# Softmax heads of groups A and C in pairs, on rows and columns of the TensorE array

## The chip, the cores and the metric

The kernel runs on one core of a Trainium2 chip. Five engines work beside each other, each through its own list of instructions: TensorE (PE; its weight loads are shown as PEld), VectorE (DVE), ScalarE (ACT), GpSimd (POOL) and SyncE (SP, which only issues DMAs here). Semaphores tie them together. The metric is the device time of one execution in microseconds (us).

## The reference, cut to what matters

One layer of a streaming encoder for 512 prompt tokens and 64 sample tokens (these with 256 cached keys). After a norm and one wide projection, three groups of heads run: A is sparse attention, B stick-breaking, C differential. The change touches A and C, whose heads have 64 features:

```python
# A, 4 heads (keys outside the chosen top-k count as masked)
logits = einsum('bthd,btkhd->bhtk', q, kg) * HEAD_DIM ** -0.5
logits = logits - slopes * dist                     # ALiBi
p = softmax(where(valid, logits, -inf)); out = p @ vg
# C, 6 heads, two maps n = 0, 1 of 32 features each
logits = einsum('bthnd,bshnd->bnhts', q, k) * DIFF_QK ** -0.5
logits = where(allowed, logits - slopes * dist, -inf)
p = softmax(logits);  w = p[:, 0] - lam * p[:, 1];  out = w @ v
oc = rmsnorm(oc) * subln * (1 - lam_init)           # per head
```

Then come the output projection with a gated residual, a router, and a mixture of 64 small experts (the longest stage, not touched). Everything is fp32; a matmul in fp32 shows in the trace as two MATMUL records, each with its own weight load.

## The kernel before, in words

The queries stand in 5 tiles: t = 0 to 3 are 128 prompt tokens each, with 128, 256, 384 and 512 keys; t = 4 are the 64 sample tokens with 320 keys. A unit is one head and one tile. `make_schedule` (lines 150 to 240) writes one list of steps, and every engine walks this list in order and does its own part of each step. So the order of the list is the order on each engine.

For a unit the steps are: `pad` (POOL copies the query rows of this head, or of this map, into a tile `q_pad` whose other rows are zero, lines 987 to 1012), `qk` (PE multiplies the padded queries, all 128 rows, by the keys of the head pair, into one PSUM bank for each map, lines 1597 to 1613), `max` (DVE adds the bias, negates, writes `p_work` and takes the row's minimum, line 2158; ACT takes the exponential and its row sum, line 1283), `norm` (DVE: a reciprocal, in C also map 1 times lambda, then the scaling or the difference, lines 2171 to 2176), `pt` (PE turns the probabilities in blocks of 128, line 1619; ACT copies them to `p_t`, lines 1295 and 1299), `pv` (PE multiplies by the values, 64 columns of the array for one head, line 1639; DVE in A and ACT in C copy the result to `o_t`). `softmax_units` staggers them: in round i stand `qk` and `max` of unit i, `norm` of i-1, `pt` of i-2 and `pv` of i-3. In A some projections (`proj`, 48 matmuls of 288 columns) and the modulation steps (`ada`, `turn`) stand between them. The weights of `proj` and `ada` come through four slots of `w_stage`; a slot of a projection is free once POOL has made `w_lo` (line 722) from ACT's `w_hi` (line 1172).

The banks of `qk` are a ring of 3 in A and of 4 in C, those of `pt` a ring of 2, and `pv` has one bank. The bias tables of C, one for each head, are made by POOL (`table`, line 984) in two slots.

The indexer's scores (step `score`, before A) multiply on 64 rows of the array without padding, even heads on rows 0 to 63, odd heads on rows 64 to 127. They and the experts' matmuls (lines 1937 and 1955, 32 columns of the array each) are the places where the kernel before uses parts of the array.

## Time and profile before

| | us |
|---|---|
| median of 3 runs (lowest, highest) | 1239.8 (1235.46, 1242.24) |
| profiled execution, its own time | 1229.7 |
| its span | 1227.7 |
| busy: PE, DVE, ACT, POOL | 1106.3, 520.7, 371.9, 367.3 |
| stage A with its projections, from its first `ada` to the last `pv` | 233 to 332.3 |
| projections, then group B | 332.3 to 434.4 |
| group C, to the first matmul of the output projection | 434.4 to 523.5 |
| output projection, router, experts, sum | 523.5 to 1227.7 |

The mean granted clock of TensorE over the span is 0.975 of full speed. In the views, a row of the timeline has the start, the time until the group's last end, the engine, the line, what is written and read, the shape (rows * columns of the array for PE), the count, and in brackets the idle time before it and its releaser. A busy time is the union of its instructions, so two that overlap count once.

### The profile page before, as it was taken

What the parts mean: (1) busy time and instruction counts of PE and PEld (TensorE: products, weight loads), DVE (VectorE), ACT (ScalarE), POOL (GpSimd) and SP (SyncE); (2) the same over time, 40 slices, a digit from 0 to 9 for tenths busy, and PEclk for the clock granted to TensorE, in tenths of its full rate; (3) what the DMA queues carried; (4) which work ended last, traced back from release to release, by engine and by line L of the source; (5) the groups of instructions that cost most, each with busy time, mean ns of one, the idle gap of its engine ahead of it and who ended that gap; (6) DMA issues with size and microseconds to landing.
All of it is one profiled execution on the core that took longest, in us unless ns stands there. A gap on an engine that the chain in (4) does not pass through costs nothing.

```text
span 1227.7 us, 24855 instructions
## 1 busy us (share of the span) xinstructions
PE 1106.3 (90%) x9769; PEld 673.1 (55%) x9769; DVE 520.7 (42%) x1293; ACT 371.9 (30%) x908; POOL 367.3 (30%) x464
## 2 busy tenths in 40 slices
PE   3899998899889988899899889999999999999696
PEld 1698896676574555545445444545555555555242
DVE  5517892133426567624552624323233332222155
ACT  3433432233335457601103212222222222222211
POOL 2233333423321043130112423434343434343100
PEclk9899999999999999999989998999999999999898
DMA  9322225633444000030054796969797969676596
GB/s 363 121 86 78 82 80 207 222 109 123 156 172 140 1 1 2 1 112 35 28 221 152 249 376 204 371 251 378 260 377 253 383 241 385 231 297 228 185 422 215
DMA packets 58563, 239.37 MB, mean 195 GB/s; under 512 B 22686, under 2 KB 22766, under 8 KB 46414
## 3 DMA queue, kind: packets, MB, share of 16 engines
q1 hardware_dynamic: 27936, 181.73, 40.2%
q0 software_dynamic: 30512, 56.06, 13.2%
q8 instruction: 78, 1.28, 0.4%
q14 instruction: 37, 0.30, 0.1%
HBM read 292.57 MB, written 47.40 MB: 277 GB/s over the span
## 4 chain that ended last, share of the span: by engine, by line
PE 68%; DMA 16%; DVE 7%; issue 4%; ACT 3%; POOL 2%; SPq 0%; POOLq 0%; DVEq 0%; ACTq 0%
PE bank L1937 14%; PE bank L1955 9%; DMA x_got<-x_dram,idx_tok 8%; PE bank L1744 6%; PE bank L1457 5%; PE bank L1459 5%; PE bank L1458 5%; DMA pairs<-pair_dram 4%; PE bank L1919 4%; PE bank L1563 3%; PE bank L1639 2%; PE bank L1485 1%; PE bank L1683 1%; PE bank L1838 1%; DMA pair_dram<-out_rows,idx_pair 1%
## 5 line engine op out<-in xcount | busy, mean ns | idle before, releaser
L1937 PE MATMUL bank<-slot,xt 128*32 128x256 f32 x4608 | 262.2, 379 | 14.9 <-issue 10.1
L1937 PEld LDWEIGHTS bank<-slot,xt 128*32 128x32 f32 x4608 | 152.5, 110 | 141.8 <-issue 54.3
L1457 PE MATMUL bank<-h_hi,w_hi 128*128 128x288 f32 x480 | 145.3, 303 | 0.0
L1458 PE MATMUL bank<-h_lo,w_hi 128*128 128x288 f32 x480 | 141.7, 295 | 0.0
L1459 PE MATMUL bank<-h_hi,w_lo 128*128 128x288 f32 x480 | 141.6, 295 | 0.0
L1955 PE MATMUL bank<-slot,hid_t 128*32 128x512 f32 x1152 | 139.2, 601 | 0.8 <-ACT hid_t L1424 0.8
L1119 POOL DMA_INDIRECT pair_dram<-out_rows,idx_pair x72 | 73.1, 1016 | 169.0 <-DVE out_rows L2429 156.1
L722 POOL TENSOR_TENSOR w_lo<-w_stage,w_hi 128x1024 fp32r<-128x1024 f32 x29 | 69.6, 2400 | 127.3 <-ACT w_hi L1172 127.3
L2429 DVE COPY out_rows<-bank 128x512 f32<-128x512 f32 x72 | 49.8, 691 | 115.3 <-PE bank L1955 75.0
L1418 ACT ACTIVATE sg<-bank 128x128 f32<-128x128 f32 x72 | 20.0, 277 | 252.0 <-PE bank L1937 251.8
L1457 PEld LDWEIGHTS bank<-h_hi,w_hi 128*128 128x128 f32 x480 | 90.5, 189 | 6.8 <-issue 6.3
L2423 DVE TENSOR_TENSOR hid<-sg,bank 128x128 f32<-128x128 f32 x72 | 20.6, 287 | 169.2 <-ACT sg L1418 160.7
L1458 PEld LDWEIGHTS bank<-h_lo,w_hi 128*128 128x128 f32 x480 | 90.6, 189 | 0.8 <-issue 0.5
L1102 POOL DMA_INDIRECT x_got<-x_dram,idx_tok x72 | 73.3, 1019 | 56.9 <-DVE idx_tok L2400 33.5
L1459 PEld LDWEIGHTS bank<-h_hi,w_lo 128*128 128x128 f32 x480 | 90.4, 188 | 0.0
L1111 POOL DMA_INDIRECT slot<-in_w_moe,idx_w x48 | 49.5, 1032 | 130.0 <-DVE out_rows L2429 76.5
L1919 PE MATMUL bank<-ident,x_got 128*128 128x128 f32 x576 | 76.3, 276 | 11.9 <-DMA x_got<-x_dram,idx_tok 11.8
L1744 PE MATMUL bank<-w_out_sb,o_t 128*128 128x512 f32 (+1 forms) x160 | 71.6, 608 | 2.5 <-DVE o_t L2189 2.5
L1919 PEld LDWEIGHTS bank<-ident,x_got 128*128 128x128 f32 x576 | 65.3, 142 | 15.2 <-DMA x_got<-x_dram,idx_tok 13.9
L1430 ACT COPY out_rows<-bank 128x512 f32<-128x512 f32 x72 | 42.2, 586 | 102.2 <-PE bank L1955 54.4
L2417 DVE COPY xt<-bank 128x512 f32<-128x512 f32 x72 | 49.8, 691 | 53.2 <-PE bank L1919 53.1
L1283 ACT ACTIVATE p_work<-p_work,n_max 128x256 f32<-128x256 f32 (+4 forms) x80 | 44.5, 557 | 62.8 <-DVE n_max L2158 62.6
(366 smaller groups left out, 1537.1 us busy)
## 6 DMA issues: line engine op xcount, KB each, us to landing
slot<-in_w_moe SPq DMA_DIRECT2D x65, 1536.0 KB, 8.7
w_stage<-in_w_ada SPq DMA_DIRECT2D x32, 512.0 KB, 4.4
pairs<-pair_dram SPq DMA_DIRECT2D x16, 1024.0 KB, 9.9
w_stage<-in_w_in SPq DMA_DIRECT2D x30, 512.0 KB, 3.3
resid<-in_w_ada SPq DMA_DIRECT2D x2, 2048.0 KB, 12.9
w_out_sb<-in_w_out SPq DMA_DIRECT2D x1, 4096.0 KB, 14.8
g_bc<-mod_dram SPq DMA_DIRECT2D x6, 512.0 KB, 8.9
o_t<-in_x_t SPq DMA_DIRECT2D x4, 576.0 KB, 5.7
```

The costliest lines, as they stand in the source:

```text
L722: e.tensor_tensor(w_lo[:, n % 2], staged(("w", n)), w_hi[:, n % 2].bitcast(F32), ALU.subtract)\
L1102: g.indirect_dma_start(x_got[:, i % 4, :], None, x_dram, bass.IndirectOffsetOnAxis(ap=idx_tok[:, i:i + 1], axis=0), bounds_check=NT - 1, o ...
L1119: g.indirect_dma_start(pair_dram, bass.IndirectOffsetOnAxis(ap=idx_pair[:, i:i + 1], axis=0), out_rows[:, i % 2, :], None, bounds_check=NT ...
L1457: mm(out, hi_w, hi_x, start=first, stop=False)
L1458: mm(out, hi_w, lo_x, start=False, stop=False)
L1459: return mm(out, lo_w, hi_x, start=False, stop=last)
L1744: ins = mm(bank[i % 4][0:n, :], o_t[:, k, c0:c0 + n], w_out_sb[:, k, 512 * c:512 * c + 512], start=(k == 0), stop=(k == KD - 1))
L1919: ins = nc.tensor.transpose(bank[k // 4][:, P * (k % 4):P * (k % 4) + P], x_got[:, i % 4, P * k:P * k + P], ident[:, :])
L1937: ins = mm(bank[2 + i % 2][r, 0:2 * P], xt[:, i % 2, k, r], slot_of(place_no)[:, 2 * P * k:2 * P * (k + 1)], start=(k == 0), stop=(k == KD ...
L1955: ins = mm(bank[4 + 2 * (i % 2) + c][r, :], hid_t[:, i % 2, r], slot_of(place_no)[:, 2 * D + 512 * c:2 * D + 512 * c + 512], start=True, s ...
L2417: v.tensor_copy(xt[:, i % 2, 4:8, :], bank[1][:, :].rearrange("p (k c) -> p k c", k=4)).then_inc(xt_dve, 1)
L2429: v.tensor_copy(out_rows[:, i % 2, 512:D], bank[5 + 2 * (i % 2)][:, :]).then_inc(out_dve, 1)
```

## The change

Two heads of one pair (2hp, 2hp+1) now go through every step together. `qk` uses each head's (A: 64 rows) or each map's (C: 32 rows) own rows of the array, straight from the projected features, so `pad`, `q_pad` and the clearing of `q_pad` are gone for A and C. `pv` does both heads, alternating between the two halves of the array's columns, and one copy moves both. Working buffers double: in C further ones lie in the features of group B (`feat2`) and in `a_t`, which are free by then. The bias tables of C have four slots, and POOL makes them earlier.

```diff
-    def softmax_units(units, fill=()):
+    def softmax_pairs(pairs, fill=()):
         fill, norms = list(fill), []
-        n = len(units)
+        n = len(pairs)
         for i in range(n + 3):
-            m = next(ada, None) if i % 4 == 0 and units[0][0] == "a" else None
+            m = next(ada, None) if i % 2 == 0 and pairs[0][0] == "a" else None
             if m is not None:
                 s.append(("ada", m))
-            if i == 0:
-                s.extend([("pad",) + units[0], ("pad",) + units[1]])
             if i < n:
-                s.append(("qk",) + units[i])
-                if i + 2 < n:
-                    s.append(("pad",) + units[i + 2])
-                s.append(("max",) + units[i])
+                s.extend([("qk",) + pairs[i], ("max",) + pairs[i]])
+            if norms and norms[0][0] == "root":
+                s.append(norms.pop(0))
...
-            if fill and i % 2 == 1:
+            if fill:
                 project([fill.pop(0)])
             if 2 <= i <= n + 1:
-                s.append(("pt",) + units[i - 2])
+                s.append(("pt",) + pairs[i - 2])
...
-            def key_products(out, q, k_new, k_old, t):
+            def key_products(parts, t):
                 rows = tokens(t)[1]
                 if t < 4:
-                    return mm(out[:, 0:keys(t)], q, k_new[:, 0:keys(t)], start=True, stop=True)
...
+                    return [mm(out[:, 0:keys(t)], q, k_new[:, 0:keys(t)], start=True, stop=True) for out, q, k_new, _ in parts]
+                for out, q, _, k_old in parts:
+                    mm(out[0:rows, 0:PAST], q, k_old, start=True, stop=True)
...
-                    for m in range(1 if g == "a" else 2):
-                        k = key + (m,)
-                        pe.wait_ge(padded, pad_no[k] + 1)
+                    c0, rows = tokens(t)
+                    for k in maps_of(key):
                         qk.wait_free(pe, k)
-                        b = qk.bank(k)
-                        key_products(score_bank[b], pad_slot(key, m)[:, 0:tokens(t)[1]], feat(SLOT["k" + g] + h // 2),
-                                     cache_t[:, cache_slot(g), h // 2, :], t).then_inc(qk_full[b], 1)
+                    done = key_products([(score_bank[qk.bank(k)], feat(SLOT["q" + g] + hp)[map_rows(k), c0:c0 + rows],
+                                          feat(SLOT["k" + g] + hp)[map_rows(k), :], cache_t[map_rows(k), cache_slot(g), hp, :])
+                                         for k in maps_of(key)], t)
+                    for k, ins in zip(maps_of(key), done):
+                        qk.fill(ins, k)
...
                     for j in range(nb):
                         w = min(P, n - P * j)
                         kt = j if t < 4 else (4 + j)
-                        ins = mm(o_bank[r, 0:rows], v_of(g)[0:w, kt, HD * h:HD * h + HD], p_t[0:w, u % 2, j, 0:rows],
-                                 start=(j == 0), stop=(j == nb - 1))
+                        for e in range(2):
+                            h, r = 2 * hp + e, slice(HD * e, HD * e + HD)
+                            ins = mm(o_bank[r, 0:rows], v_of(g)[0:w, kt, HD * h:HD * h + HD], turned_at(key, e)[0:w, j, 0:rows],
+                                     start=(j == 0), stop=(j == nb - 1), skip_group_check=True)
...
-                    v.tensor_copy(o_t[r, MIX[g] + h // 2, c0:c0 + rows], o_bank[r, 0:rows]).then_inc(o_free, 1)
+                    v.tensor_copy(o_t[:, MIX[g] + hp, c0:c0 + rows], o_bank[:, 0:rows]).then_inc(o_free, 1)
...
-                if step == ("pad", "c", 0, 0):
+                if step == ("z", "s", 0, 2):
                     qk.wait_full(pool, ("b", H_B - 1, 0))
                     table(0)
-                if step[0:2] == ("max", "c") and step[3] == 2 and step[2] < H_C - 1:
-                    table(step[2] + 1)
+                    table(1)
+                if step == ("qk", "c", 0, 0):
+                    qk.wait_full(pool, stick_key[len(stick_no) - 1])
+                    table(2)
+                    table(3)
+                if step == ("max", "c", 1, 1):
+                    table(4)
+                    table(5)
```

`maps_of(pair)` lists the maps of both heads: two in A, four in C. With four, a pair takes all four banks of the ring at once. `map_rows` gives the rows of a map. The step `root` (ACT) is now placed right behind `max`, and the scaling of `o_t` by the norm, which was DVE's part of `root`, is a step `scale` of its own.

PE in group C, before: heads 3 and 4, tiles 3, 4 and 0 in turn. Line 1563 to 1565 are `qk`, 1619 is `pt`, 1639 is `pv`.

```order
L1563 MATMUL bank<-resid,a_t 128x512 x2
L1619 MATMUL bank<-ident,p_work 128x128 x2
L1639 MATMUL bank<-p_t,v_rows 64x128
L1564 MATMUL bank<-cache_t,a_t 64x256
L1565 MATMUL bank<-resid,a_t 64x64
L1564 MATMUL bank<-cache_t,a_t 64x256
L1565 MATMUL bank<-resid,a_t 64x64
L1619 MATMUL bank<-ident,p_work 128x128 x3
L1639 MATMUL bank<-p_t,v_rows 64x128 x2
L1563 MATMUL bank<-resid,a_t 128x128 x2
```

PE in group C, changed: the pair of heads 2 and 3, tiles 3, 4 and then the next pair's tile 0. Lines 1579 to 1582 are `qk`, 1640 is `pt`, 1662 is `pv`; `feat` and `resid` hold features, and `feat` here also stands for the further buffers.

```order
L1579 MATMUL bank<-resid 128x512 x4
L1640 MATMUL bank<-ident,p_work 128x128 x2
L1640 MATMUL bank<-ident,a_t 128x128 x2
L1662 MATMUL bank<-feat,v_rows 64x128 x2
L1671 MATMUL bank<-sp_buf,two_heads 128x512
L1674 MATMUL bank<-sp_buf,two_heads 128x64
L1581 MATMUL bank<-cache_t,resid 64x256 x4
L1582 MATMUL bank<-resid 64x64 x4
L1640 MATMUL bank<-ident,feat 128x128 x6
L1662 MATMUL bank<-p_t,v_rows 64x128 x4
L1579 MATMUL bank<-resid 128x128 x4
```

Before, two matmuls of one head's maps stand between two turns. Now four stand in a row, then both heads' turns, then both heads' products with the values.

DVE in group C, before: `max` of one unit (line 2158, one ISA row for each map and one for its minimum), then `norm` of the unit before it.

```order
L2158 ISA p_work,n_max<-bank,bias 128x256 [waits p_ready,qk_full0,tr_full1,bias_ready]
L2158 ISA n_max 128x1
L2158 ISA p_work,n_max<-bank,bias 128x256 [waits qk_full1]
L2158 ISA n_max 128x1
L2171 RECIPROCAL p_rec<-p_sum 128x2 [waits p_ready,exp_ready]
L2175 TENSOR_SCALAR p_work<-p_work,p_rec,lam 128x128 [waits dve_step]
L2176 SCALAR_TENSOR_TENSOR p_work<-p_work,p_rec 128x128 [waits dve_step]
```

DVE in group C, changed, the same tiles: `max` of a pair, then `norm` of the pair before it.

```order
L2183 ISA p_work,n_max<-bank,bias 128x256 [waits p_ready,qk_full2,tr_full1,bias_ready]
L2183 ISA n_max 128x1
L2183 ISA p_work,n_max<-bank,bias 128x256 [waits qk_full3]
L2183 ISA n_max 128x1
L2183 ISA p_work,n_max<-bank,bias 128x256 [waits p_ready,qk_full0,tr_full0,bias_ready]
L2183 ISA n_max 128x1
L2183 ISA p_work,n_max<-bank,bias 128x256 [waits qk_full1]
L2183 ISA n_max 128x1
L2198 RECIPROCAL p_rec<-p_sum 128x2 [waits p_ready,exp_ready]
L2202 TENSOR_SCALAR feat<-feat,p_rec,lam 128x128 [waits dve_step]
L2203 SCALAR_TENSOR_TENSOR feat<-feat,p_rec 128x128 [waits dve_step]
```

The work per head is the same; it comes in groups of four maps and then two norms (of which the first is shown).

## Rows read from the trace of the kernel before

**Rows 1.** Windows, stages A and C: length, busy by engine, PEclk, DMA share, GB/s.

```profile
233.00:332.30 99.30, 90.83 (x601) 64.98 (x599) 39.46 (x129) 33.98 (x90) 32.01 (x41) 0.98 0.42 144
...
434.40:523.50 89.10, 73.63 (x393) 46.59 (x392) 62.28 (x214) 59.82 (x198) 28.95 (x67) 0.97 0.00 1
```

**Rows 2.** Waits, 434 to 524: waiter, releaser, total us, times, longest.

```profile
PEld bank L1619 <- DVE p_work L2176: 11.7, 15, 1.4
...
DVE p_work L2158 <- PE bank L1563: 9.0, 12, 1.0
```

**Rows 3.** Timeline of PE: start, length, line, operands, rows*columns, shape, count.

```profile
138.51 0.70 PE L1563 MATMUL bank<-resid 64*128 64x512 f32 x2
```

**Rows 4.** The same view of PE at 508 to 517: 512-column products, and P by V.

```profile
508.30 1.98 PE L1563 MATMUL bank<-resid,a_t 128*128 128x512 f32 x4
...
516.48 1.06 PE L1639 MATMUL bank<-p_t,v_rows 128*64 128x128 f32 x8
```

**Rows 5.** Groups of PE by form: count | busy us, mean ns | idle before.

```profile
L1955 PE MATMUL bank<-slot,hid_t 128*32 128x512 f32 x1152 | 139.2, 601 | 0.8 <-ACT hid_t L1424 0.8
...
L1563 PE MATMUL bank<-resid 64*128 64x512 f32 x16 | 5.9, 634 | 0.0
```

**Rows 6.** Timeline of DVE in C, where it hardly waits.

```profile
458.78 0.47 DVE L2158 CUSTOM_DVE_ANT_0 p_work<-bank,bias 64x320 f32<-64x320 f32 x1
...
459.60 0.15 DVE L2171 RECIPROCAL p_rec<-p_sum 128x2 f32<-128x2 f32 x1
459.78 0.55 DVE L2175 TENSOR_SCALAR p_work<-p_work,p_rec,lam 128x512 f32<-128x512 f32 x1
460.37 0.75 DVE L2176 SCALAR_TENSOR_TENSOR p_work<-p_work,p_rec 128x512 f32<-128x512 f32 x1
461.03 0.28 DVE L2158 CUSTOM_DVE_ANT_0 p_work<-bank,bias 128x128 f32<-128x128 f32 x1
...
464.13 0.16 DVE L2171 RECIPROCAL p_rec<-p_sum 128x2 f32<-128x2 f32 x1
...
464.71 0.35 DVE L2176 SCALAR_TENSOR_TENSOR p_work<-p_work,p_rec 128x128 f32<-128x128 f32 x1
```

**Rows 7.** Timeline of all engines, the start of C.

```profile
434.63 0.95 POOL L995 MEMSET a_t<- 128x1024 f32 x1 [25.86 <-PE bank L1720]
...
436.53 1.52 POOL L984 TENSOR_SCALAR bias<-dist 128x512 f32<-128x512 f32 x1 [0.19 <-POOL a_t L1012]
438.08 0.29 DVE L2158 CUSTOM_DVE_ANT_0 p_work<-bank,bias 128x128 f32<-128x128 f32 x1 [3.11 <-POOL bias L984]
```

**Rows 8.** The same view, the end of C: last norm, first output product.

```profile
515.11 0.54 DVE L2176 SCALAR_TENSOR_TENSOR p_work<-p_work,p_rec 64x320 f32<-64x320 f32 x1
...
523.50 1.19 PE L1744 MATMUL bank<-w_out_sb,o_t 128*128 128x512 f32 x1 [2.49 <-DVE o_t L2189]
```

**Rows 9.** Chain that ended last, stage A: start, length, what.

```profile
235.53 0.29 POOL a_t L1012
...
251.08 3.57 DMA w_stage<-in_w_ada
254.79 3.61 PE bank L1485 x16
...
281.50 1.85 PE bank L1485 x16
...
310.70 1.98 PE bank L1485 x16
...
320.98 2.02 PE bank L1485 x16
...
332.32 0.80 PE bank L1583 x6
```

**Rows 10.** Windows around the start of C, columns as in rows 1.

```profile
435.70:439.10 3.40, 1.34 (x7) 1.13 (x8) 0.51 (x4) 0.69 (x3) 2.88 (x6) 1.00 0.00 0
439.10:442.50 3.40, 3.40 (x9) 1.93 (x8) 2.24 (x10) 1.96 (x8) 1.13 (x6) 0.51 0.00 0
```

More of the change, by code:

```diff
@@ L238, in make_schedule @@
     assert next(ada, None) is None
-    softmax_units([("c", h, t) for h in range(H_C) for t in range(5)])
+    softmax_pairs([("c", hp, t) for hp in range(H_C // 2) for t in range(5)])
     return s
@@ L588, in build, with maps_of @@
         o_uses, n_o = {}, 0
+        def maps_of(pair):
+            g, hp, t = pair
+            return [(g, 2 * hp + e, t, m) for e in range(2) for m in range(2 if g == "c" else 1)]
         for n in range(N_FIRST):
@@ new lines, in _ @@
+                    for k in maps_of(key):
+                        qk.wait_taken(act, k)
+                        w, i, m = map_at(k)[0:rows, 0:n], stat(key, k[1] % 2), k[3]
+                        nc.scalar.activation(w, w, ACT.Exp, scale=-1.0, bias=n_max[0:rows, i, m:m + 1],
+                                             accum_out=p_sum[0:rows, i, m:m + 1]).then_inc(exp_ready, 1)
+                elif kind == "pt":
+                    g, hp, t = key
+                    rows, n = tokens(t)[1], keys(t)
+                    if pair_no[key] >= 2:
+                        act.wait_ge(o_full, pair_no[key] - 1)
@@ new lines, in _ @@
+                    for k, ins in zip(maps_of(key), done):
+                        qk.fill(ins, k)
+                elif kind == "pt":
+                    g, hp, t = key
+                    rows, n = tokens(t)[1], keys(t)
+                    for e in range(2):
+                        pe.wait_ge(p_ready, 2 * pair_no[key] + e + 1)
+                        tr.wait_free(pe, step + (e,))
+                        out, p = tr_bank[tr.bank(step + (e,))], map_at((g, 2 * hp + e, t, 0))
+                        for j in range((n + P - 1) // P):
+                            w = min(P, n - P * j)
+                            ins = nc.tensor.transpose(out[0:w, rows * j:rows * j + rows], p[0:rows, P * j:P * j + w],
+                                                      ident[0:rows, 0:rows])
+                        tr.fill(ins, step + (e,))
@@ L2162, in _ @@
                 elif kind == "norm":
-                    g, h, t = key
-                    rows, n, u = tokens(t)[1], keys(t), unit_no[key]
+                    g, hp, t = key
+                    rows, n, i = tokens(t)[1], keys(t), pair_no[key]
                     maps = 2 if g == "c" else 1
-                    dve.wait_ge(exp_ready, map_no[key + (maps - 1,)] + 1)
-                    e = [p_work[0:rows, 2 * (u % 3) + m, 0:n] for m in range(2)]
-                    rec = p_rec[0:rows, u % 2, :]
```

297 lines of the change are left out of this document (143 added, 154 removed).

## The prediction

> **What bounds the kernel now.** I read the busy time of each stage first, then who waits for whom, then single instructions. The stages that the change touches are A and C [rows 1]. In A PE is busy 90.8 of 99.3 us and DVE 39.5: A is bound by PE, with two kinds of pause, for weights and for turned rows. In C it is a tie: PE 73.6, DVE 62.3, ACT 59.8 of 89.1 us. PE waits for DVE's probabilities 15 times (11.7 us), DVE waits for PE's products 12 times (9.0 us) [rows 2]. So in C both take turns at being late, and neither is full. The reader is to see that C has about 89 - 62 = 27 us to give before DVE is full, and A about 99 - 40 before anything but PE and its weights counts.
>
> Can parts of the array work side by side? Rows first. Four products of 512 columns on 128 rows take 1.98 us [rows 4]; one alone lasts 0.70 [rows 3], so from start to start it is (1.98 - 0.70) / 3 = 0.427, one behind the other. Two on 64 rows, heads 0 and 1 of the indexer, start together and last 0.70 in all [rows 3], where one behind the other would need 0.43 + 0.70. That is two row halves at once, into two banks. On columns: 1152 products of 512 columns on 32 array columns each take 139.2 us [rows 5], 0.121 each, so 3.5 of them run at once. Four row quarters, and two column halves with fp32 and 128 tokens, no row shows; their nearest rows are these.
>
> **The change, part by part.** The sum goes against the profiled execution (span 1227.7, its own time 1229.7, 2.0 around the span). The median of the three runs is 1239.8, 0.8% above it; I scale at the end.
>
> *QK.* 0.427 for 512 columns is 0.834 ns a column, two records a map, 1600 columns a head over its five tiles: 2.67 us. A: 4 heads, 10.7 us, halved: -5.3. C: 12 maps, 32.0 us, at four abreast 8.0: -24.0 of PE work. Bounds: -24 (four abreast), 0 (one after another).
>
> *PV.* Eight records last 1.06, some 0.11 each [rows 4]; a head has 26 records (20 of 128 tokens, 6 of 64), 2.5 us. A: 9.9 us, halved -5.0. C: 14.8 us, -7.4. Bounds: half, or nothing. I take half: the experts' columns reach 3.5 of 4.
>
> *Pads.* POOL's copies and clearing go. On the path they stand once in each stage: PE's first QK of A waited some 0.5 us for them (the copy at 235.53, rows 9), and in C POOL cleared (0.95 from 434.63), padded and made a table (1.52) before DVE could begin at 438.08 [rows 7]. The tables of heads 0 and 1 are now made during the last steps of B, where POOL had been idle 25.9 us. DVE should begin right after its last copy of B, at about 435.0: -3.1 us.
>
> *A, as a path.* PE is the bound, so I walk from one `ada` to the next [rows 9]. First to second (to 254.79): the two QK halvings (2 x 0.43) and 0.5 of padding are saved. The turns of the first pair move behind. But `ada` 8 needs its fourth slot, and this waits for `w_lo` of projection 23, which starts only after ACT's exponentials of pair 1; then 1.0 (`w_hi`) + 2.4 (`w_lo`) + 3.6 (DMA, the 251.08 row). I get about 253.1: -1.7, and a PE pause of about 2.6 in place of 1.9. Second to third (26.7 us): four QK become two (-1.3), PV halves (-1.2 to -1.9), fewer pauses between groups: -3.4. Third to fourth (29.2): -1.7 in QK, -1.7 in PV: -3.8. Fourth to fifth (10.3): -2 of PE work, but all four slots of the next `ada` are loaded after the former one has run, in some 8 us, and DVE's share for tiles 3 and 4 comes close: -1.1. Fifth to the end (11.3): chains of tile 0 through DVE and ACT: -1.0. Sum -11.0; PE work plus padding alone is 5.3 + 5.0 + 0.5 = 10.8. I take -10.5. Bounds: -5 (only halves of it reach the path), -12.
>
> *C, as a path.* PE's 73.6 busy us lose over 30, so DVE sets the pace: 62.3 busy [rows 1]. Its order is `max` of pair i, then `norm` of pair i-1. A pair takes all four banks, so QK of the next pair starts only after DVE has read the last one. What hides it is `norm`: for a 512-column head 0.18 + 0.59 + 0.66 = 1.43, so 2.9 a pair, and for a 128-column one 0.58 + 0.35 = 0.93, so 1.9 a pair [rows 6]. QK of a pair needs about 2 x 0.43 + 0.3 = 1.15 us at 512 columns and less elsewhere: hidden. If the cover goes, each us of QK above `norm` is a us of DVE's waiting. DVE's path: start 435.0; 0.9 bare QK in front of the second pair; 62.3 less 0.4 (the copy of B before the start) and 0.8 (the last scaling, which is in the tail); small gaps, 0.04 between chained instructions and 0.1 to 0.2 of semaphore waits a pair, together 4.5; last norm ends at 501.5. The tail from there to the output products was 523.50 - 515.65 = 7.85 [rows 8] and has the same links: 509.4. That is -14.1. ACT comes close behind: 59.8, less 15 of its 30 copies of 0.26, is 56; its exponentials of one pair have a `norm` and the next `max` to finish. For waits that these two hand each other, and for a slower PE (below), I take 1.1 off: -13. Bounds: -16.5 (no gap; DVE's operations shorter without POOL's copies beside them), -6 (first rival).
>
> Sum: -10.5 - 13 = -23.5. 1229.7 - 23.5 = 1206.2, a ratio of 0.981; on the median 1216. After C everything only moves forward: the loads of the experts' weights are issued behind the end of C in the same lists.
>
> **Clock.** Behind a stretch in which PE was busy only 1.34 us (435.7 to 439.1), it was granted 0.51 of full speed from 439.1 to 442.5, that is 1.2 GHz, busy all the time [rows 10], and then 2.4 GHz again. In C now PE would have some 73.6 - 31 = 42 us of 74, in short bursts, so I expect 1.2 GHz in a third or more of C. At that level QK of 512 columns lasts about 2.0 against a norm of 2.5 or more over 256 columns: still hidden; turns and PV of a wide tile that stand before QK are late behind a narrow `max`, 1 to 1.5 us a head pair, up to 4 us in all. The Trainium skill ("TensorE: Matmul & The Clock Gate", section "HAM oscillation — how this bites in real kernels") says that pauses of PE drop its clock and that bursts shorter than the waits begin cold each time. That speaks against the change; by that rule C would run at 1.2 GHz nearly throughout, the same up to 4 us.
>
> The Trainium skill also has a price for four row quarters ("TensorE: Matmul & The Clock Gate", "Measured speedup vs the span model"): 3.07 times, not 4. An estimate by that page makes QK of 512 columns 1.4 in place of 1.15 us, hidden all the same; no run here shows it yet.
>
> **The rivals.** (1) *Row quarters don't run abreast*, at 2.4 GHz. For: only halves are shown. Against: rows 3, and 3.5 column quarters in rows 5. Then QK of a C pair takes 1.0, 2.0, 2.9, 3.7 and 2.4 us for the five tiles and sticks out over `norm` by 1.2 at tile 2 and 1.6 at tile 3: 2.8 x 3 = 8.4 us. C gives about 6, A 9: with A's halves still abreast -15, and 1225 on the median. If halves fail too, -11 and 1229.
> (2) *The clock costs more*: C at 1.2 GHz with late turns, and cold `ada` steps in A (the one at 254.79 took 3.61 where others take 1.9, rows 9) twice more. 4 + 3.5 us: -17, 1223.
> (3) *DVE waits for QK in every pair, slower than before.* One mechanism, in C between `max` of a pair and `max` of the next: the four maps one behind another at 1.2 GHz. QK would take 2.0, 3.7, 5.4, 7.1 and 4.6 us against norms of 1.9 to 2.9, 12 us a head pair beyond the cover, 36 in all, and turns 9 more: C +31, A -8, 1263. It decides once QK sticks out by more than 1.6 us a pair on average (23.5 / 15). Against: a PE that busy keeps its clock.
> (4) *The gain isn't there*: B or the experts' loads give it back. Against: B is not touched, and DMA share is 0.00 in C [rows 1]. 1238.
>
> **Chances.** Forecast 0.58, (1) 0.15, (2) 0.18, (3) 0.04, (4) 0.05. The forecast's own range is 1211 to 1221 (A -9 to -12, C -10 to -16.5). To hold 8 in 10 it must take in (2), and (1) in part: 1207 to 1228. What this kernel's measurement can tell from no change is about 0.5%, 6 us: faster 0.91, within 0.05, slower 0.04.
>
> **What would show it.** In C: the four QK records of a pair start within some 0.1 us; DVE is busy over 80% of C, with its first `max` near its last copy of B; C lasts 74 to 78 us; PEclk well below 0.97 there. In A: PV records in twos; `ada` 8 still waits for its DMA. Wrong would be: QK records 0.4 apart, DVE waiting for PE once a pair, ACT full instead of DVE, or A shortened by less than 5 us.

## The result, and the profile after

The changed kernel takes 1227.4 us (median of 21 runs, 1215.8 to 1240.0), the kernel before, run beside it, 1240.3 (21 runs, 1234.3 to 1250.8). The ratio is 0.9889, with a 95% interval of 0.9865 to 0.9914: 13.8 us less. (The ratio leaves out 4 of the 21 runs of the changed kernel as being in a slower state of the chip; the medians of all runs are 12.9 us apart.) The forecast was 23.8 less (1216), with a range of 1207 to 1228. The profiled execution took 1222.9, its span is 1221.1 (before 1227.7).

I read the two touched stages first, A in the first row and C in the second, as in [rows 1] (length, busy time of PE, PEld, DVE, ACT, POOL, PEclk, DMA share, GB/s), of the changed kernel:

```profile
235.50:327.90 92.40, 79.67 (x601) 56.77 (x599) 35.69 (x119) 34.21 (x90) 24.84 (x20) 0.97 0.46 155
434.00:508.70 74.70, 49.21 (x396) 29.52 (x393) 60.29 (x214) 53.95 (x183) 3.17 (x2) 0.78 0.00 1
```

A went from 99.3 to 92.4, C from 89.1 to 74.7. Together that is 21.3 us. In C PE has a third less to do (73.6 to 49.2), DVE has nearly all that it had, and it is now the busiest engine. That answers the first question of the forecast: DVE now sets the pace of C. The next is whether the row quarters run abreast; the timeline of PE in the changed C shows QK of a 512-column pair, and P by V of a four-block pair:

```profile
485.59 1.14 PE L1579 MATMUL bank<-resid 32*128 32x512 f32 x8 [0.80 <-DVE n_max L2183]
...
501.56 1.09 PE L1662 MATMUL bank<-feat,v_rows 128*64 128x128 f32 x16
```

Eight records in 1.14 us, where four took 1.98 [rows 4]; sixteen of P by V in 1.09, where eight took 1.06. Both are what the forecast assumed. The start and the end of C, as in [rows 7] and [rows 8]: the first maximum, the last two `norm` products, the last scaling, and the first output product.

```profile
434.82 0.29 DVE L2183 CUSTOM_DVE_ANT_0 p_work<-bank,bias 128x128 f32<-128x128 f32 x1 [0.19 <-PE bank L1579]
...
498.63 0.54 DVE L2203 SCALAR_TENSOR_TENSOR p_work<-p_work,p_rec 64x320 f32<-64x320 f32 x1
...
499.76 0.54 DVE L2203 SCALAR_TENSOR_TENSOR p_work<-p_work,p_rec 64x320 f32<-64x320 f32 x1
...
507.76 0.82 DVE L2215 SCALAR_TENSOR_TENSOR o_t<-o_t,vec,rstd 128x576 f32<-128x576 f32 x1 [7.46 <-ACT rstd L1177]
...
508.68 1.19 PE L1767 MATMUL bank<-w_out_sb,o_t 128*128 128x512 f32 x1 [2.49 <-DVE o_t L2215]
```

And who waits for whom in C now, against [rows 2]:

```profile
DVE o_t L2215 <- ACT rstd L1177: 7.5, 1, 7.5
PE bank L1640 <- ACT log_ms L1343: 6.8, 2, 3.4
PE bank L1579 <- DVE n_max L2183: 6.8, 7, 1.7
...
DVE feat L2183 <- PE bank L1579: 2.2, 2, 1.2
```

DVE waits for PE some 4 us in all (the row shown and two of 1.6 and 0.5) in place of 9.0 and more; PE waits for DVE. The 7.5 stand in the tail. Two waits of 3.4 us are new on PE: ACT's logarithm for the group norm now comes behind the next pair's exponentials.

In A the chain ends as follows in the changed kernel (compare [rows 9]): the loads for the last `ada`, the product itself, the turn of the cache.

```profile
302.93 1.98 PE bank L1501 x16
...
306.52 8.05 DMA w_stage<-in_w_ada
314.71 2.53 PE bank L1501 x16
...
327.95 1.47 PE bank L1601 x6
```

The same `ada` in the timeline of PE, with its wait:

```profile
314.71 2.46 PE L1501 MATMUL bank<-w_stage,silu_c 128*32 128x512 f32 x16 [2.32 <-DMA w_stage<-in_w_ada]
```

Start by start, beside [rows 9] (233.7 the first): 20.1, 21.4, 25.1, 11.9 and 13.2 us, where before had 21.0, 26.6, 29.2, 10.3 and 11.3. The first three steps are 10.2 shorter, the last two 3.5 longer. A part of the 3.5 is the clock: from 316.0 to 319.4 us it was granted at half.

How does the work go on behind A? The first row is the changed kernel from the turn of the cache on, the second the same stretch of the kernel before; both are full of projections, and PE waits in neither.

```profile
327.90:331.30 3.40, 3.40 (x17) 3.40 (x16) 0.29 (x1) 1.81 (x3) 2.16 (x5) 0.50 0.39 112
```

```profile
332.30:335.70 3.40, 3.40 (x28) 3.40 (x28) 0.29 (x1) 1.81 (x3) 2.65 (x5) 1.00 0.37 115
```

The changed kernel comes out of A at half clock, which lasts from 326.2 to 333.0. I come back to it below.

So much for what was touched. The rest was to stay as it was. In the profiled executions it did not: up to the start of A +2.5, between A and C +4.0, output projection and routing +0.4, experts +4.3, the last sums +3.6. That is 14.8 of the 21.3, and 6.5 are left of the span. The timed runs, which are many, leave 13.8. What of these 14.8 belongs to the change was a question for the experiments.

### The profile page after: what moved, and what is told of

It reads as the page before. It is cut to its first block, busy times and chain, and to the rows that moved or that the text cites. A ratio compares the mean times of both kernels' runs of the same rounds, so it can differ in the third digit from the quotient of the medians.

```text
span 1221.1 us, 24577 instructions
## 1 busy us (share of the span) xinstructions
PE 1081.2 (89%) x9769; PEld 652.2 (53%) x9769; DVE 515.5 (42%) x1283; ACT 365.8 (30%) x893; POOL 340.0 (28%) x382
## 3 DMA queue, kind: packets, MB, share of 16 engines
q0 software_dynamic: 30512, 56.06, 13.2%
## 4 chain that ended last, share of the span: by engine, by line
PE 67%; DMA 17%; DVE 6%; issue 4%; ACT 3%; POOL 1%; SPq 0%; DVEq 0%; POOLq 0%; ACTq 0%
PE bank L1960 14%; DMA x_got<-x_dram,idx_tok 9%; PE bank L1978 9%; PE bank L1767 6%; PE bank L1473 5%; PE bank L1475 5%; PE bank L1474 5%; PE bank L1942 4%; DMA pairs<-pair_dram 4%; PE bank L1579 2%; PE bank L1501 2%; DMA w_stage<-in_w_ada 2%; PE bank L1706 1%; PE bank L1861 1%; PE bank L1640 1%
## 5 line engine op out<-in xcount | busy, mean ns | idle before, releaser
L1960 PE MATMUL bank<-slot,xt 128*32 128x256 f32 x4608 | 262.1, 379 | 10.5 <-issue 7.4
L1978 PE MATMUL bank<-slot,hid_t 128*32 128x512 f32 x1152 | 141.8, 611 | 0.7 <-ACT hid_t L1440 0.7
L1473 PEld LDWEIGHTS bank<-h_hi,w_hi 128*128 128x128 f32 x480 | 91.4, 190 | 10.2 <-issue 10.0
L1942 PE MATMUL bank<-ident,x_got 128*128 128x128 f32 x576 | 77.6, 279 | 17.9 <-DMA x_got<-x_dram,idx_tok 17.9
L1942 PEld LDWEIGHTS bank<-ident,x_got 128*128 128x128 f32 x576 | 66.6, 144 | 20.6 <-DMA x_got<-x_dram,idx_tok 19.4
L1978 PEld LDWEIGHTS bank<-slot,hid_t 128*32 128x32 f32 x1152 | 30.5, 111 | 58.5 <-issue 57.4
```

The costliest lines, as they stand in the source:

```text
L1473: mm(out, hi_w, hi_x, start=first, stop=False)
L1942: ins = nc.tensor.transpose(bank[k // 4][:, P * (k % 4):P * (k % 4) + P], x_got[:, i % 4, P * k:P * k + P], ident[:, :])
L1960: ins = mm(bank[2 + i % 2][r, 0:2 * P], xt[:, i % 2, k, r], slot_of(place_no)[:, 2 * P * k:2 * P * (k + 1)], start=(k == 0), stop=(k == KD ...
L1978: ins = mm(bank[4 + 2 * (i % 2) + c][r, :], hid_t[:, i % 2, r], slot_of(place_no)[:, 2 * D + 512 * c:2 * D + 512 * c + 512], start=True, s ...
```

## The experiments

Stage lengths, each from one profile, A and C measured as above. (The expectations count A from the start of the first `ada` itself, 0.7 us less than the table: 91.7 for the changed kernel.) The time is a median where there are several runs. What repeats of the same code show is the noise of a stage: A has the changed kernel's code in five kernels (changed, once more, `root` first and the two with extra products) and takes 91.0 to 92.4; C of the changed kernel took 74.7 and 75.5. In the four kernels with "all rows" or "same rows" the products read other rows than they should, so their results are not those of the layer; only their times are of use.

| kernel | time us (runs) | ratio to before | A | C | PEclk in C | PE busy in C | last sums |
|---|---|---|---|---|---|---|---|
| before | 1240.3 (21) | 1 | 99.3 | 89.1 | 0.97 | 73.6 | 62.0 |
| before once more | 1236.3 (1) | | 97.6 | 89.8 | | | 62.0 |
| changed | 1227.4 (21) | 0.9889 [0.9865, 0.9914] | 92.4 | 74.7 | 0.78 | 49.2 | 65.6 |
| changed once more | 1227.4 (6) | 0.9858 [0.9813, 0.9902] | 92.0 | 75.5 | 0.75 | 50.1 | 66.9 |
| `root` first | 1226.1 (4) | 0.9854 [0.9806, 0.9902] | 92.3 | 74.4 | 0.75 | 50.6 | 65.9 |
| `root` first, last `ada` later | 1224.3 (6) | 0.9843 [0.9805, 0.9881] | | 76.7 | | | 65.9 |
| own rows alone | 1266.0 (4) | 1.0204 [1.0150, 1.0257] | 100.6 | 108.3 | 0.56 | 99.9 | 66.0 |
| no pads, all rows | 1229.9 (1) | | 97.3 | 86.9 | 0.96 | 74.1 | 65.6 |
| pairs, all on the same rows | 1248.3 (1) | | 92.7 | 104.6 | 0.62 | 94.3 | 65.6 |
| pairs, all rows | 1226.6 (1) | | 93.5 | 78.0 | 0.93 | 64.0 | 65.6 |
| pairs, all rows, P by V in turn | 1221.5 (1) | | 93.2 | 80.5 | 0.95 | 66.6 | 67.3 |
| pairs, P by V in turn | 1225.3 (1) | | 92.3 | 77.1 | 0.76 | 53.7 | 65.8 |
| extra products before the turns | 1226.8 (4) | 0.9881 [0.9821, 0.9940] | 91.0 | 77.5 | 0.88 | 59.4 | 62.3 |
| extra product behind QK | 1220.6 (4) | 0.9853 [0.9803, 0.9903] | 91.6 | 77.5 | 0.85 | 55.2 | 61.9 |

**Both kernels once more.** No edit.

> The changed kernel once more, for a second profile. In the first, stage C (last product of B to the output projection) took 74.7 us against 89.2 before, as forecast; A gave 6.8 instead of 10.5, the projections and B behind it were 4.0 us longer though nothing in them changed, and the stages after C 8.2 us longer. Theory 1: the losses in A and B belong to the change (modulation step 11 waits for its weights, TensorE falls to 1.2 GHz, the next projections' weights come late) and repeat here: from the ada step before (10) to step 11 11.5 to 12.5 us, first to second projection behind A 10 to 11 us; the 8 us behind C do not repeat (the output projection to the end within 3 us of before's second profile). Theory 2: the loss behind C belongs to the change: the experts' stage is 4 us longer again. Time: ratio 0.989 as before.

> The kernel before, once more, for a second profile of its stages. Theory 1: A 98 to 99 us, C 89 us, from the projections behind A to the end of B 102 us, from there within 0.5 us of the first profile; the stages behind C differ from the first profile by several us, since their time depends on the DMA and not on the change. Theory 2: they come out at 704 us again, within 1 us, and 712 in the changed kernel is then the change's doing.

C and A came out again (74.7 and 75.5; 92.4 and 92.0), but in the kernel before A was 97.6 instead of 99.3: its second `ada` was not at half clock this time. In the changed kernel it was the other way round: half clock there in the second profile and not in the first. The experts' stage was 508.4 and 515.7 us in the same kernel. So a difference of 4 us between two profiles of that stage says nothing, and 1.7 of A's 6.9 was luck of the first profile.

**`root` in front of the next pair's exponentials.**

```
+            if norms and norms[0][0] == "root":
+                s.append(norms.pop(0))
             if i < n:
                 s.extend([("qk",) + pairs[i], ("max",) + pairs[i]])
-            if norms and norms[0][0] == "root":
-                s.append(norms.pop(0))
```

> The changed kernel with one step moved: the logarithm and root of the norm (root, ACT) stand ahead of the pair's exponentials and not behind them. In the changed kernel the turned-rows bank that the norm's sums fill is held until ACT reads it behind four exponentials, PE waits 3.4 us for it twice, and DVE stands 1.2 and 1.1 us behind each. Theory 1: PE's wait for log_ms falls from 6.8 us to under 2, C from 74.7 to 70 to 71 us, the time by 4 us (ratio to before 0.985 to 0.987). Rival: the clock or ACT sets C, and moving the step only moves the wait: C 74 to 75.

The two waits of 3.4 us went (one of 2.2 for the logarithm is left), C stayed (74.4), as the rival said. These waits of PE were free, since DVE sets the pace.

**And the last `ada` behind A.** The same edit, and

```
-            m = next(ada, None) if i % 2 == 0 and pairs[0][0] == "a" else None
+            m = next(ada, None) if i % 2 == 0 and i < 8 and pairs[0][0] == "a" else None
...
-    project(TILES[27:])
+    project(TILES[27:29])
+    n = next(ada)
+    s += [("ada", n), ("turn", n)]
+    project(TILES[29:])
```

> The changed kernel with root ahead of the exponentials, and the last modulation step (ada 11 with its turn) moved from the eighth pair of A to a place between the second and third projection behind A, where its weights are long there. Theory 1 (A's end waits for these weights): A, from its first ada to the turning of C's cached keys, falls from 91.7 to 84 to 86 us, of which 3 come back in the projections behind it; the projections' weights are no longer late (first to second 7.6 us and not 9.4); with root's 4 us the whole is 6 to 9 us faster than the changed kernel, ratio to before 0.981 to 0.984. Rival (the chain through DVE and ACT sets A's end, the weights only stand beside it): A falls by no more than the 3 us that move out, and the whole by 4 us.

A, counted as in the expectation, took 85.9 us. From the fourth `ada` of A to the turn of the cache it was 17.9 us in place of 23.3 to 25.1. From there to the end of B it took 110.1 in place of 106.1 and 106.3 (the two changed profiles). Some 4 of the 5.4 to 7.2 us were given back at once (3 had been expected, for the step that moved), and the ratio, 0.9843, can't be told from that of the changed kernel.

**Each map on its own rows, heads one by one as before.**

```
-            if st[0] == "pad":
+            if st[0] == "pad" and st[1] == "b":
...
-                        key_products(score_bank[b], pad_slot(key, m)[:, 0:tokens(t)[1]], feat(SLOT["k" + g] + h // 2),
-                                     cache_t[:, cache_slot(g), h // 2, :], t).then_inc(qk_full[b], 1)
+                        r = pad_rows(key, m)
+                        key_products(score_bank[b], feat(SLOT["q" + g] + h // 2)[r, c0:c0 + rows],
+                                     feat(SLOT["k" + g] + h // 2)[r, :], cache_t[r, cache_slot(g), h // 2, :], t).then_inc(qk_full[b], 1)
```

> The kernel before with one part of the change: each map's product reads its own rows of the queries and keys (64 in A, 32 in C) and the padded copies of groups A and C go; heads are still taken one by one, P by V as before. Theory (both parts are needed: C is paced by DVE only once four maps run at once): in C the two maps of a head run at once, 16 of its 32 us of QK go, the first max comes 3 us earlier; PE 73.6 - 16 = 58 busy, DVE 62; C 80 to 83 us in place of 89.2, A 98 in place of 98.6 (one map a head, nothing beside it), in all 7 to 9 us off. Rival (the rows bring it all, pairing is only a form): C 75 to 77, 13 us off. Second rival (what ends the chain is the norm, not PE): C 86, only the 3 us of its start.

All three expectations failed: the kernel is 2% slower, and C takes 108.3 us. The windows of C in this kernel show why (all of it; the part at one clock):

```profile
442.10:550.40 108.30, 99.94 (x394) 57.20 (x392) 62.62 (x214) 59.99 (x198) 6.95 (x4) 0.56 0.00 1
447.20:542.80 95.60, 92.78 (x352) 53.34 (x352) 57.33 (x194) 53.22 (x176) 6.95 (x4) 0.50 0.00 1
```

PE is busy 92.8 of 95.6 us and is granted half its clock all the time. The fall itself came as in [rows 10], behind a stretch with pauses (PE busy 2.03 of the 3.40 us before 447.2). But there full clock came back after 3.4 busy us, and here 95.6 us of a busy PE did not bring it back.

**All maps of a pair on the same rows** (0 to 31 in C, 0 to 63 in A).

```
-            w = QK_C if g == "c" else HD
-            return slice(HD * (h % 2) + w * m, HD * (h % 2) + w * m + w)
+            return slice(0, QK_C if g == "c" else HD)
```

> The changed kernel with all maps of a pair read from the same rows (0 to 31 in C, 0 to 63 in A), so that their products can't run side by side: the scores of the other heads and maps are computed from the first one's features, everything else is as in the changed kernel. Theory (row quarters bring what C gains): four QK of 512 columns start some 0.43 us apart at full clock, 0.85 at half; C 84 to 92 in place of 74.7; A 4 to 6 us longer than 91.7. Rival (C's gain comes from the order in pairs, the missing pads and the P by V halves): C stays within 77. Third view, my priced rival of serial maps at half clock: C 110 and more.

Now the timeline of PE shows one product behind the other, at half clock. A window inside C shows a PE that hardly pauses, and two later ones, next to each other, show the clock fall from full to half while PE is busy without a pause:

```profile
471.27 7.19 PE L1578 MATMUL bank<-resid 32*128 32x512 f32 x8
```

```profile
436.70:464.00 27.30, 27.17 (x85) 15.32 (x86) 18.18 (x61) 13.60 (x47) 3.17 (x2) 0.50 0.00 1
...
467.40:470.80 3.40, 3.40 (x20) 1.85 (x18) 2.82 (x11) 2.62 (x10) 0.00 (x0) 1.00 0.00 0
470.80:474.20 3.40, 3.40 (x14) 1.66 (x9) 2.62 (x8) 1.93 (x8) 0.00 (x0) 0.50 0.03 7
```

The eight records start 0.85 us apart, twice the 0.43 of full clock, so PE is really full and not just shown as busy. 7.19 us, and in the changed kernel, side by side and at full clock, 1.14. C is 104.6. A, where QK on 64 rows is serial too, is 92.7 in place of 92.4: nothing.

**All 128 rows, in pairs, and without pads in the order of before.** In the changed kernel `return slice(0, P)` for the rows, which makes every score a sum over the tile's maps; in the kernel with each map on its own rows, one head at a time, `r = slice(0, P)` in place of `r = pad_rows(key, m)`.

> The changed kernel with every map's product read over all 128 rows of queries and keys (the scores are then sums over the pair's maps; everything else as in the changed kernel). It is as serial as the run in which all maps used the same 32 rows, where C lasted 104.6 us at a granted clock of 0.62 with PE busy 94.3. Theory A (the clock fell there because the products stood on few rows): with 128 rows the clock of C is 0.9 or above, PE is busy some 75 us, C lasts 80 to 87. Theory B (it fell through the pauses between the bursts, or through the order in pairs): clock 0.6 again, C 100 to 107. In A stage (64 rows before) nothing moves: 92.

> The kernel before without the padded copies of A and C, each product read over all 128 rows of the features (scores are sums over the heads and maps that share a tile; the order and all else as before). Against the run with own rows (C 108.3 us, clock 0.55, PE busy 99.9) only the rows of the products differ. Theory A (rows set the clock): clock 0.95, C 85 to 88, that is 89.2 less the 3.1 us of its start; A 98 to 99. Theory B (the missing pads let something start in another rhythm and the clock falls by that): clock below 0.7, C above 100.

Theory A held both times (C of the run in pairs came out 2 us under its range). Only the rows of the QK products differ between 108.3 us at 0.56 and 86.9 at 0.96, or between 104.6 at 0.62 and 78.0 at 0.93. The windows of C in the run in pairs, and its QK of 512 columns:

```profile
437.60:515.60 78.00, 63.95 (x395) 41.92 (x392) 60.97 (x214) 54.33 (x183) 3.17 (x2) 0.93 0.00 1
```

```profile
465.79 3.70 PE L1578 MATMUL bank<-resid 128*128 128x512 f32 x8
```

3.70 us, one behind the other at full clock, against 1.14: the quarters run 3.2 times as fast. And yet C is just 3.3 us longer (78.0 to 74.7). DVE takes the maps one by one. Its timeline in the changed kernel shows the last instruction of `norm` over 256 columns, which stands in front of a 512-column `max`, and the first two maps of this `max`:

```profile
487.05 0.48 DVE L2203 SCALAR_TENSOR_TENSOR p_work<-p_work,p_rec 128x256 f32<-128x256 f32 x1
487.45 0.68 DVE L2183 CUSTOM_DVE_ANT_0 feat<-bank,bias 128x512 f32<-128x512 f32 x1
...
488.06 0.69 DVE L2183 CUSTOM_DVE_ANT_0 feat<-bank,bias 128x512 f32<-128x512 f32 x1
```

That is one map every 0.61. QK of this pair began at 485.59, so DVE came to the first map 1.86 us later and to the fourth 3.69 us later, and by then even serial products are done (3.70). In the run over all rows DVE does not wait at any 512-column tile. Its longest waits beside the tail and the start of C are two at the sample tokens' tile, of which this is one:

```profile
499.75 0.48 DVE L2182 CUSTOM_DVE_ANT_0 p_work<-bank,bias 64x320 f32<-64x320 f32 x1 [1.45 <-PE bank L1581]
```

There `key_products` issues the cached parts of all four maps first and the new parts after them, so no map is complete early. In the changed kernel these waits are 0.25. In all, DVE waits for QK 7.0 us in place of 4.3 and is busy 0.7 longer.

**P by V with the heads in turn**, alone and on top of all rows.

```
-                    for j in range(nb):
...
-                        for e in range(2):
+                    for e in range(2):
+                        for j in range(nb):
```

> The changed kernel with the P by V products of a pair in another order: all blocks of the first head, then all of the second, each still on its own half of the columns. Theory (neighbouring instructions on different column halves run side by side): sixteen records of a pair last 2.1 us in place of 1.09, A 3 to 5 us longer than 91.7 and C within 1 us of 74.7, since DVE paces it. Rival (the halves never ran side by side, records are just shorter): sixteen still last 1.1 and nothing moves.

> The changed kernel with QK over all 128 rows and, in P by V, all blocks of the first head before those of the second. The question is A: with QK alone made serial it took 91.9, with P by V alone 91.6, the changed kernel 91.7. Theory A (A is bound by the weights' loads, its gain is from the order in pairs and the missing pads, and PE's saved work lies in pauses): A 92 to 93.5 again. Theory B (each of the two halves alone fills the pauses that the other leaves, both together show): A 95 to 98. C: as the run with full rows, plus up to 7 us if PE is its bound there.

P by V of three blocks in A, by the timeline of PE: one head in the kernel without pads; then two heads in turn; then two heads block by block, in the changed kernel. The row of the kernel without pads:

```profile
297.01 0.87 PE L1635 MATMUL bank<-p_t,v_rows 128*64 128x128 f32 x6
```

In turn (the run with P by V alone in turn; the second row has four blocks):

```profile
300.24 1.15 PE L1662 MATMUL bank<-p_t,v_rows 128*64 128x128 f32 x12
...
310.01 1.58 PE L1662 MATMUL bank<-p_t,v_rows 128*64 128x128 f32 x16
```

Block by block:

```profile
302.05 0.88 PE L1662 MATMUL bank<-p_t,v_rows 128*64 128x128 f32 x12
```

The halves do run side by side: two heads in the time of one. But in turn they need 1.15 for twelve records and 1.58 for sixteen, not the 2.1 that I expected for sixteen: the second head's first record starts 0.28 us behind the first head's, amid its records. Two heads in one group overlap already in part, whatever the order inside. In A the halves count for little: 92.3 with P by V in turn, 92.7 with QK on the same rows, 93.5 with QK over all rows, 93.2 with both undone (theory A; the 95 of theory B is far). C has 77.1 with P by V in turn, 2.4 more than the changed kernel, where I expected at most 1; 1.7 of this is in the tail, from the last `norm` to the output product (10.1 in place of 8.4). With both undone C is 80.5.

**Extra products, to lift the clock in C.** Two of 512 and 256 columns ahead of the turns of 13 pairs; or, in another kernel, one of 512 behind QK of 12, whose edit is this:

```
+                    if g == "c" and at not in (0, 8, 13):
+                        if at in (9, 14):
+                            pe.wait_ge(log_ready, 3 if at == 9 else 4)
+                        mm(bank[0][:, 0:512], ident[:, :], dist[:, 0:512], start=True, stop=True)
```

> The changed kernel with two extra products of 512 and 256 columns behind each pair's turns in C (13 of 15 pairs), whose results nobody reads: 0.64 us of PE each at full clock, 8 us in all. Theory (the granted clock of 0.78 in C costs time): with PE busier the clock stays at 0.9 or above and C takes 72 to 73 in place of 74.7. Rival (DVE paces C, the clock costs it nothing): clock up, C 74 to 76. Third: the extra work does not lift the clock and delays the turns, C 77 to 80.

> The changed kernel with one extra product of 512 columns on 128 rows behind QK of 12 of the 15 pairs of C, where PE would wait for DVE, its result unread: 5.1 us of PE at full clock. Two extra products ahead of the turns gave clock 0.88 and C 77.5, but they stood in the way of the turns. Theory (the low clock costs C time): clock 0.85 or above and C 72 to 74. Rival (DVE, 60.3 of 74.7 us busy and waiting for PE only some 4 us, paces C): C 74 to 76 whatever the clock.

The clock rose (0.88 and 0.85, from 0.78), C did not shrink: 77.5 both times, for the first kernel the length of the third theory with the clock of the first, for the second longer than either gave. The waits of DVE tell where the 2.8 us are. In the kernel with products ahead of the turns:

```profile
DVE o_t L2221 <- ACT rstd L1177: 10.1, 1, 10.1
```

With the product behind QK:

```profile
DVE o_t L2220 <- ACT rstd L1177: 8.7, 1, 8.7
...
DVE feat L2188 <- PE bank L1579: 4.4, 2, 3.4
```

The first has 2.6 more in the tail, the second 1.2 there and 2.2 behind a product that itself waits for the logarithm. In the first kernel's loop nothing changed: length less DVE's busy time less the tail's wait is 74.7 - 60.3 - 7.5 = 6.9 in the changed kernel and 77.5 - 60.2 - 10.1 = 7.2 at the higher clock. So lifting the clock by extra work brings nothing here; that the work itself takes back what the clock gives is not excluded.

The low clock is not free all the same. Two kernels have the same code in C, `root` first and the one with the last `ada` later: 74.4 at a clock of 0.75, and 76.7 at 0.65. Of these 2.3 us, 1.2 are waits of DVE before the tail. In the kernel with 76.7 the tail ran at half clock from end to end:

```profile
502.06:511.98 9.92, 6.04 (x37) 3.95 (x36) 0.82 (x2) 3.57 (x10) 0.00 (x0) 0.50 0.00 1
```

The changed kernel's tail, nearly all at full clock, lasts 8.4 (500.31 to 508.68, clock 0.91). So what half clock costs C in these runs is up to 2 us, as against a spread of 0.8 between the two profiles of the changed kernel.

## Why the prediction came out as it did

**What held.** The mechanism and the size of C: -14.4 measured, -13 forecast (74 to 78 us). Its walk gave the first maximum at 435.0, the last norm at 501.5, the output product at 509.4; the trace has 434.82, 500.30 and 508.68. PE's clock, expected at 1.2 GHz "in a third or more", was there for 44% of C (0.78), and what I took off for it and for other waits (1.1 us) was enough. The estimate of 1.4 us for QK of 512 columns was too long: it is 1.14. One reading was off without harm: I had `norm` over 256 columns at "2.5 or more"; a pair's lasts 2.1 (485.36 to 487.45), which just covers QK of 512 columns at half clock (1.8 to 2.1).

**What C's gain is made of** was told wrong. The forecast put four maps abreast first (-24 us of PE work). Undone, they cost 3.3 us of C. The runs without own rows divide the 14.4 so: missing pads and an earlier start 2.2 (89.1 to 86.9), heads in pairs 6.4 (86.9 to 80.5, with QK serial and one head's P by V behind the other's in both), P by V block by block 2.5 (80.5 to 78.0), maps abreast 3.3 (78.0 to 74.7). Each is a difference of single profiles, good to some 0.8 us. The earlier start alone was forecast at 3.1, and without pads the first `max` did come 2.9 sooner; but the tail is 1.7 longer (9.5 in place of 7.85), at a clock of 0.68. In my rival (1) I let the whole of a pair's QK stick out over `norm`, 8.4 us; DVE needs only the first map at that point and the others later, so it is 3.3.

**Why own rows were dangerous.** Against my slow rival (3) I wrote "a PE that busy keeps its clock". That is false here: 27.17 of 27.30 us busy at 0.50 with QK on 32 rows (turns and P by V are the same in every kernel, on 64 or 128 rows), 0.93 to 0.96 for the whole of C when QK stands on 128. The rival's mechanism is the run with the same rows: its QK was 7.19 us as I had priced it (7.1), its C 104.6 and not 120, again since DVE takes map by map. The padded rows of the kernel before, which look like waste, held its clock at 0.97. It is the rows that count and not the zeros: without pads, but over all 128 rows, it is 0.96. With each map on its own rows and without pairs the kernel is 2% slower. With pairs the change gets away with it: PE has half clock in 44% of C, and mostly still keeps ahead of DVE. The Trainium skill ("TensorE: Matmul & The Clock Gate", section "HAM oscillation — how this bites in real kernels") has pauses as the cause of a drop. The rows above show a drop without a pause (470.8) and a busy PE whose clock does not come back, and there the measurement decides. Why few rows matter was not found out, and how much of the changed kernel's 0.78 comes of few rows and how much of its pauses is not divided.

**A** gave 6.9 of 10.5, and of these 1.7 are a slow `ada` in the profile before. The step that failed is "PE is the bound, so I walk from one `ada` to the next" with half of QK (5.3) and half of P by V (5.0) as what is saved: with both undone A is only 0.8 longer. What shortens A is the pair as such: 97.3 without pads in the order of before, 93.2 in pairs with everything serial. P by V accounts for it, and its price was too low (9.9 us of work forecast for A). From the start of a group to the next thing on PE, pauses included, summed over A, it takes 16.0 us one head at a time and 10.3 in pairs in turn; the rows above show it for one step, twice 0.87 against 1.15. The first three terms of the walk were right in sum (-8.9 forecast; -10.2 measured, of which 1.7 are the slow `ada`). The mis-sized terms are the last two. Fourth to fifth `ada`: -1.1 forecast, +1.6 measured, and +1.3 in the second profiles of both kernels. I had the loads of "some 8 us" right (8.05) and contradicted them: with the `ada` before them (1.9) they make 9.9 of the 10.3 that the step had, so it could not shrink by 1.1. PE waits 2.3 us for them. Fifth to the end: -1.0 forecast, +1.9 measured in the first profiles, but +0.3 in the second ones, where the clock was full at that place; in the first the fifth `ada` took 2.53 in place of 1.98.

**"After C everything only moves forward", and "B is not touched".** This is the other step that failed, or at least can't be upheld. Between A and C the changed profile has 106.1 in place of 102.1. 2.4 of it come before the second projection there, and they are the clock: PE does not wait, it works at half clock until 333.0 (the two windows under the result), behind 3.40 us in which it was busy 2.24. That alone does not decide it: in the kernel before PE was busy 2.26 of the last 3.40 us of A, and its clock stayed full. The five profiles whose clock is full there (before twice, without pads, and of the pairs P by V in turn and everything serial) take 8.2 us from the turn of the cache to the second projection, the nine with a spell at half clock 9.4 to 10.7: own rows alone, and eight of the ten in pairs. 1.7 are in B, where PE waits 2.3 us for a table of POOL in every kernel. In the kernel before full clock follows:

```profile
358.99 0.88 PE L1663 MATMUL bank<-feat,bias 128*128 128x384 f32 x2 [2.35 <-POOL bias L1012]
```

In the changed kernel, half clock, with the windows around it:

```profile
356.99 1.62 PE L1686 MATMUL bank<-feat,bias 128*128 128x384 f32 x2 [2.34 <-POOL bias L1025]
```

```profile
353.50:356.90 3.40, 1.14 (x9) 0.74 (x7) 1.30 (x4) 2.02 (x6) 1.62 (x3) 1.00 0.75 279
356.90:360.30 3.40, 3.31 (x8) 2.22 (x9) 1.55 (x5) 1.03 (x3) 0.87 (x3) 0.50 1.00 366
```

Counted from the second projection to the end of B it lasts 93.8 to 94.2 where this drop is missing (both profiles of before, the two unpaired kernels, but also three in pairs) and 95.3 to 96.6 where it comes (six of the kernels in pairs and none of the others; the one whose last `ada` runs behind A isn't counted). The pause is the same in all; why the clock falls behind it in some kernels only was not tested.

The last sums took 62.0 twice in the kernel before and 65.6 in the changed one. The waits of PE for the last rows of this stage, in the changed kernel:

```profile
PE bank L2010 <- DMA pairs<-pair_dram: 4.0, 1, 4.0
```

In the kernel without pads, whose code behind C is that of before:

```profile
PE bank L1983 <- DMA pairs<-pair_dram: 4.1, 1, 4.1
```

The kernel before has 2.4 there, in two waits. Behind the wait of 4.0 the sums go on at half clock for 3.4 us (1203.4 to 1206.8), and behind the two shorter ones at full clock, which is the other half of the 3.6 us. So the late landing is not the change's: it comes in two unpaired kernels (65.6, 66.0) and is missing in two in pairs (62.3, 61.9). What decides it stays open.

**The sum.** 21.3 us were won in A and C by the first pair of profiles, 19.6 without the slow `ada`; the timed runs keep 13.8 [10.7 to 16.7]. Some 6 us are thus returned outside. In the first profile 2.4 in front of the second projection and 1.7 in B can be named, both at half clock; the rest lies within what the experts' stage and the last sums differ by in unchanged code, and no run here divides it. The two kernels in pairs with serial products have C and A together 4.4 us longer (all rows) and 6.6 us longer (everything serial) than the changed kernel, and yet single times of 1226.6 and 1221.5. For the second, 3.7 us come back between A and C, where its clock did not fall; one run each proves no more. None of the variants beats the changed kernel by more than the intervals.

**How much of the hit is luck.** The time, 1227.4, is 0.6 us inside the range and outside the forecast's own 1211 to 1221. The range reached so far up for the rivals (1), quarters that don't run abreast, and (2), a dearer clock in C and in the `ada` steps. (1) did not happen. Of (2) the kind of cost came, but elsewhere: behind A and in B. And (4), "B gives it back", came in part with 1.7 us. So the mechanism of C was right, and that the whole time lies in the range rests on width that was meant for other causes.

## What to carry to other kernels

Before pricing a saving on one engine, ask in what portions the next engine takes it: the last of a pair's products came 2.6 us sooner, and DVE, which takes them one by one, came to it no sooner than the serial one would have been there. Two units handled as one group can bring more than the parallel hardware that they were paired for. And when products are put on fewer rows, look at the granted clock of a stage in which PE is full: rows that pad a product to 128 may be what keeps the clock up. Look, too, at the clock of the untouched work behind the stage that you changed: in most of these kernels it began at half clock, and no wait shows that.

## What was not expected of the hardware

- QK on 32 rows between turns and P by V on 64 or 128, PE busy 97% of 95.6 us: granted clock 0.50 throughout. The same stage with QK over 128 rows: 0.96. In A, with 64-row products among projections, 0.97 (changed) and 0.98 (own rows, one head at a time).
- With QK on 32 rows the clock also fell behind 3.40 us in which PE was busy all the time (467.4 to 470.8).
- Four products on four row quarters, fp32, 512 columns: 1.14 us against 3.70 one behind the other, 3.2 times.
- Two heads' P by V on two column halves: 0.88 us block by block, 1.15 one head behind the other, 0.87 for one head alone (three blocks each).
- Untouched code at the end had two outcomes, 61.9 to 62.3 us for the last sums in four profiles and 65.6 to 67.3 in ten; the kernel before had the same one twice, the changed kernel too.
